# A large expert asks for its width once instead of three times, on TensorE's instruction stream

## What is computed

```python
logits = xf @ w_router + b_router              # 264 tokens of width 1024 (the meta tokens' rows are dropped)
top_val, top_idx = top_k(logits, 4)            # 4 of 32 experts for each token
gates = softmax(top_val)
# for each expert e, over the tokens that chose it:
gt  = minimum(x @ w_gate[e] + b_gate[e], 7)
up  = clip(x @ w_up[e] + b_up[e], -7, 7)
hdn = (up + 1) * gt * sigmoid(1.702 * gt)
out += gate * (hdn @ w_down[e] + b_down[e])
```

## Time and profile before

| what | us |
| --- | --- |
| median of 3 runs | 1245.64 (1241.58 to 1249.92) |
| the profiled execution | 1245.33 |
| its span, first to last instruction | 1243.4 |
| TensorE busy | 1160.7 |
| VectorE busy | 448.6 |
| ScalarE busy | 197.8 |
| mean granted TensorE clock | 0.977 |

### The profile page before, as it was taken

One profiled execution on the slowest core, in us unless ns is written; L12 is line 12 of the kernel. 1 busy time (PEld: TensorE's weight loads), 2 busy tenths in 40 slices (PEclk: granted clock), 3 DMA queues, 4 the chain that ended last, 5 costly groups with the idle time before them and its releaser, 6 DMA issues.

```text
span 1243.4 us, 20526 instructions
## 1 busy us (share of the span) xinstructions
PE 1160.7 (93%) x8392; PEld 550.3 (44%) x8392; DVE 448.6 (36%) x1031; ACT 197.8 (16%) x435; POOL 5.8 (0%) x34
## 2 busy tenths in 40 slices
PE   8999989999999979898999999999999999999886
PEld 6888767774334323232333433333343334343333
DVE  2999998214332323121311233111232212222224
ACT  2234504121110111111110011100111001111012
POOL 1000000000000000000000000000000000000000
PEclk9999999999989999989999999999999899999989
DMA  9641328936989999999999999999999999999993
GB/s 393 239 173 68 144 110 332 370 144 253 381 357 426 427 426 425 427 427 424 426 426 427 425 426 425 427 425 402 427 426 427 424 427 388 429 425 425 429 425 153
DMA packets 37074, 452.62 MB, mean 364 GB/s; under 512 B 5112, under 2 KB 5656, under 8 KB 10080
## 3 DMA queue, kind: packets, MB, share of 16 engines
q1 hardware_dynamic: 35344, 449.02, 86.5%
q10 hardware_dynamic: 1616, 1.82, 0.4%
HBM read 443.57 MB, written 7.25 MB: 363 GB/s over the span
## 4 chain that ended last, share of the span: by engine, by line
PE 55%; DMA 29%; DVE 13%; issue 1%; DVEq 1%; ACT 0%; POOL 0%; SPq 0%; POOLq 0%; ACTq 0%
DMA ring<-in_w_experts 28%; PE ps L1597 23%; PE ps L1630 9%; DVE acts L794 5%; PE ps L1348 3%; PE ps L1523 2%; PE ps L1640 2%; PE ps L1322 2%; PE ps L1564 2%; PE ps L1645 2%; PE ps L1579 2%; DVE acts L889 1%; PE ps L1652 1%; PE ps L1464 1%; PE ps L1620 1%
## 5 line engine op out<-in xcount | busy, mean ns | idle before, releaser
L1597 PE MATMUL ps<-ring,extra 128*64 128x512 f32 x1824 | 415.4, 609 | 18.6 <-DMA ring<-in_w_experts 18.1
L1597 PEld LDWEIGHTS ps<-ring,extra 128*64 128x64 f32 x1824 | 128.8, 140 | 292.1 <-issue 256.3
L1630 PE MATMUL ps<-ring,extra 128*32 128x256 f32 x3072 | 189.3, 388 | 18.7 <-DMA ring<-in_w_experts 18.4
L1630 PEld LDWEIGHTS ps<-ring,extra 128*32 128x32 f32 x3072 | 91.6, 111 | 111.6 <-issue 37.3
L1119 DVE TENSOR_TENSOR acts<-ps,acts 128x528 f32<-128x528 f32 x68 | 47.8, 707 | 252.9 <-PE ps L1645 232.1
L1124 DVE TENSOR_SCALAR extra<-ps 128x512 f32<-128x512 f32 x32 | 22.1, 692 | 216.5 <-PE ps L1597 216.5
L794 DVE SCALAR_TENSOR_TENSOR acts<-ring,small,acts 128x256 f32<-128x256 f32 x224 | 91.4, 478 | 1.1 <-ACT acts L500 1.1
L1348 PE MATMUL ps<-acts,ring 128*128 128x280 f32 (+1 forms) x320 | 75.3, 395 | 0.3 <-ACT ring L573 0.3
L1348 PEld LDWEIGHTS ps<-acts,ring 128*128 128x128 f32 x320 | 60.6, 190 | 14.1 <-issue 1.0
L1348 PE MATMUL ps<-acts,extra 128*128 128x280 f32 x256 | 61.3, 400 | 1.9 <-DVE acts L776 1.9
L1133 DVE TENSOR_SCALAR extra<-ps 128x512 f32<-128x512 f32 x32 | 22.1, 689 | 100.9 <-PE ps L1597 83.1
(11 more groups left out here) (315 smaller groups left out, 854.5 us busy)
## 6 DMA issues: line engine op xcount, KB each, us to landing
ring<-in_w_experts SPq DMA_DIRECT2D x192, 2048.0 KB, 28.9
ring<-in_w_in_t SPq DMA_DIRECT2D x5, 2048.0 KB, 20.9
extra<-in_w_in_t SPq DMA_DIRECT2D x4, 2048.0 KB, 10.9
extra<-in_w_out_t SPq DMA_DIRECT2D x4, 1024.0 KB, 5.9
ring<-in_w_out_t SPq DMA_DIRECT2D x4, 1024.0 KB, 6.1
ring<-in_state_t SPq DMA_DIRECT2D x8, 512.0 KB, 8.8
ring<-dtx_rows SPq DMA_DIRECT2D x8, 512.0 KB, 8.2
out_ssm_s_t<-ring SPq DMA_DIRECT2D x8, 512.0 KB, 8.0
```

What stands on the lines that cost most here:

```text
L1597: hs.append(MM(dst, src[:, o:o + HALF], weight(w, p, k, 512 * h_, 512), start=(fresh and kk == 0), stop=(kk == KT - 1), skip_group_check=T ...
L1630: hs.append(MM(dst, src[:, o:o + QUAR], weight(w, p, k, 256 * q, 256), start=(fresh and kk == 0), stop=(kk == KT - 1), skip_group_check=True))
```

## The change

In a large expert that has a small one behind it, everything from the gate to the down products is put into one function of the width, `whole(n)`, and the width is asked for once. In expert 0, which has a large one behind it, the questions stay as they were. In a small expert, the gather, the turn of its own hidden rows, the slot pick and the turn of the next one's inputs are put into one function `prepare(n)` of the next one's width, asked for once; the operations and waits keep their order. Only TensorE's stream changes.

```diff
-                by_width(count, gate_up)
-                if i == 0:
+                def rest(n):
+                    pe.wait_ge(ev["s_ready"], i + 2)
+                    pe.wait_ge(ev["y_back"], i * 2 + 64)
+                    gather_s()
+                    turn_hidden(n, i * 2)
+                    pe.wait_ge(ev["p_ready"], i + 1)
+                    if i == 1:
+                        pe.wait_ge(ev["acc_done"], back_no(i) + 4)
+                    pick_slots()
+                    pe.wait_ge(ev["xg_out"], i * 2 + 4)
+                    turn_s(xg, 2, ev["xt_done"])
+                    down_of(n, i * 2, w)
+
+                def whole(n):
+                    gate_up(n)
+                    rest(n)
+
+                if following is None:
+                    by_width(count, whole)
+                else:
+                    by_width(count, gate_up)
                     find_order()
                     pe.wait_ge(ev["xg_out"], 2)
-                pe.wait_ge(ev["s_ready"], i + 2)
-                pe.wait_ge(ev["y_back"], i * 2 + 64)
-                if following is None:
-                    gather_s()
-                else:
+                    pe.wait_ge(ev["s_ready"], i + 2)
+                    pe.wait_ge(ev["y_back"], i * 2 + 64)
                     by_width(following, lambda n: gather(n, True))
-                by_width(count, lambda n: turn_hidden(n, i * 2))
-                pe.wait_ge(ev["p_ready"], i + 1)
-                if i == 0:
+                    by_width(count, lambda n: turn_hidden(n, i * 2))
+                    pe.wait_ge(ev["p_ready"], i + 1)
                     pe.wait_ge(ev["order_ready"], 1)
-                elif i == 1:
-                    pe.wait_ge(ev["acc_done"], back_no(i) + 4)
-                pick_slots()
-                if following is None:
-                    pe.wait_ge(ev["xg_out"], i * 2 + 4)
-                    turn_s(xg, 2, ev["xt_done"])
-                else:
+                    pick_slots()
                     pe.wait_ge(ev["hdn_ready"], i * 2 + 2)
                     by_width(following, turn_next(i))
-                by_width(count, lambda n: down_of(n, i * 2, w))
+                    by_width(count, lambda n: down_of(n, i * 2, w))
                 pe.wait_ge(ev["ht_ready"], i * 2 + 2)
...
                 pe.wait_ge(ev["s_ready"], i + 2)
+
+                def prepare(n):
+                    if following is None:
+                        gather_s(False)
+                    else:
+                        gather(n)
+                    pe.wait_ge(ev["hdn_ready"], i * 2 + 2)
+                    turn_s(hdn, 0, ev["ht_done"])
+                    pe.wait_ge(ev["acc_done"], back_no(i) + 4)
+                    pick_slots()
+                    if following is None:
+                        pe.wait_ge(ev["xg_out"], i * 2 + 4)
+                        turn_s(xg, 2, ev["xt_done"])
+                    else:
+                        turn_next(i)(n)
+
                 if following is None:
-                    gather_s(False)
+                    prepare(1)
                 else:
-                    by_width(following, gather)
-                pe.wait_ge(ev["hdn_ready"], i * 2 + 2)
-                turn_s(hdn, 0, ev["ht_done"])
-                pe.wait_ge(ev["acc_done"], back_no(i) + 4)
-                pick_slots()
-                if following is None:
-                    pe.wait_ge(ev["xg_out"], i * 2 + 4)
-                    turn_s(xg, 2, ev["xt_done"])
-                else:
-                    by_width(following, turn_next(i))
+                    by_width(following, prepare)
                 down_s(i * 2, w)
```

## The result

The changed kernel takes 1262.43 us (median of 4 runs, 1251.94 to 1267.56) beside 1245.59 us for the kernel before: a ratio of 1.0134, interval 1.0104 to 1.0164, so 16.8 us and 1.3% slower. The forecast was 1243 in 1236 to 1255; what came is the rival "the cover runs out", worked out as 1264. The profiled execution is the shortest of the four (1251.94 us, span 1250.0, mean granted clock 0.985).

The account below looks back on a forecast made before the run. The prediction took the experts' weight stream, 424 to 427 GB/s, as the bound, with the engine behind only in wide stretches. 1245.3 - 4.1 + 1 + 1 = 1243.2, with the runs' median 0.3 higher; forecast 1243, range 1236 to 1255.

Parts of the forecast that it names:

- the cover runs out: Rival: stalls with half clock make narrow pairs 56.2 us, leaving 22.9 us of lag at the end; 1264 us, chance 0.13.
- The bound and the mechanism: Whole kernel: weight stream bounds, branches cost 0, jumps past the next instruction block stall, 1.75 to 2.97 us in 12 experts.
- First term, the early gain: Around 352 us: without expert 1's stall before its gather, a buffer frees earlier and the dry stream closes; gain 4.1 us.
- Second term, the middle: Narrow and wide pairs: narrow pairs with stalls still make good a wide pair's 14.4 us lag; +1 us (0 to 5).
- The 4.6 us in hand before the stream stops: Behind expert 24: a pair lands 12.5 us after issue, 7.9 with an empty queue, so 4.6 us of slack.
- from 3.0 us a stall on: The rival's threshold: from this stall length two narrow pairs no longer make good a wide one.
- Third term, the end: Experts 26, 28 and 30: three stalls, some 6 us, may make the engine later than the stream; +1 us (0 to 4).

Follow-up runs that it names:

- e2: The kernel before with only the small experts' half of the change; large ones ask as before: 1243.59 us, ratio 0.9988.
- e8: The kernel before with the large experts' gate and up products cut into parts, no jump passing over more than 128 instructions: 1240.68 us, ratio 0.9961.
- e7: The kernel before with never-executed matmuls added, so narrow experts from 4 on jump some 500 instructions ahead of the gather: 1255.78 us, ratio 1.0116.
- e3: The kernel before with the large experts' half of the change in expert 1 only: 1242.24 us, ratio 0.9995.
- e12: The changed kernel with the width test's bound at 256 slots, so every large expert takes the narrow version: 1241.34 us, ratio 0.9977.
- e5: The kernel before with the large experts' half of the change in experts from 14 on only: 1265.95 us, ratio 1.0197.
- e4: The kernel before with the large experts' half of the change in experts 1 to 10 only: 1243.31 us, ratio 1.0000.
- e9: The kernel before with the width test's bound at 320, above the declared 264, so every large expert is worked as narrow: 1233.92 us.
- e11: The kernel before with the width test's bound at 256 slots, so every large expert takes the narrow version: 1243.07 us, ratio 0.9982.
- e13: The kernel before with short jumps in the large experts' gate and up products plus the small experts' half of the change: 1241.33 us, ratio 0.9972.

## Why the prediction was wrong

**The bound and the mechanism** were right. The stream was the bound with the engine close behind. A taken branch costs nothing visible by itself (e2, and e8 with more of them), a long jump waits for its block (e7, e8), and the new stalls lie ahead of the small expert's first products, none ahead of a gather. The Trainium skill, "Runtime: NRT & Kernel Launch", Instruction fetch mechanics, says that a taken branch to a target outside the window of two blocks has to wait for the target's block. The runs agree: waits behind 6 of 13 jumps over 280 instructions (1.1 blocks), behind all 11 over some 500 in e7, and none in e8.

**First term, the early gain.** Forecast 4.1 us, with SP's issue near 349. In place of the earlier trace rows stands

```profile
347.16 0.34 SPq L398 DMA_DIRECT2D ring<-in_w_experts  x1
```

8.1 us earlier and before the queue was empty; the gather started right behind the up products. The stretch lost 6.1 us less, of which 1.7 went again behind expert 12. The term was right in its sign, but e3 could not show it in the time.

**Second term, the middle: this is the step that failed.** "Before, two narrow pairs regained 20.5; now 14.4 to 16.8. That just suffices before the next wide one", and +1 us was taken. The traced execution lost 15.7 us more stream behind the wide experts. What the pairs regained, measured: 55.6 + 61.2 = 116.8 us for the two pairs ahead of expert 18, so 118.2 - 116.8 = 1.4 us regained of 14.4; and 55.8 + 57.1, so 5.3 regained ahead of 24. Four things were mis-sized or left out:
- Waits for issue per pair: 1.8 to 3.0 forecast; 4.6, 6.3, 3.8 and 3.7 found. The second wait behind a landing near a block's end was thought of for the last experts only ("perhaps a second wait"). A wait within the small expert came behind six of the twelve landings.
- The lower clock next to the waits. It was put into the rival alone, on the word of expert 26, where a 1.75 us wait had no such fall. The pair of expert 16, with a clock of 0.94, has 2.3 us of it: 61.2 is 48.9, 6.3 of waits, 3.7 of the next point and 2.3 more. That of expert 20, also 0.94, has 55.8 - 48.9 - 3.8 = 3.1.
- The small expert ahead of a wide one gathers and turns twice as much. The second gather block is 2.9 us, the turns and the wait for their input 0.8 to 0.9. The 48.9 us came from a pair with a narrow one behind it. So 3.7 of the 20.5 us in hand were never there, and of the 6.1 us that seemed left over after the wide pair's 14.4 only 2.4 were. The trace of the kernel before shows it as well: its pair 16 and 17, from 755.56 to 812.41, takes 56.9 us, of which 2.6 are a wait for weights and 1.4 the half clock behind it; 52.9 remain. First these rows of before, then those of after, ahead of a narrow expert and ahead of wide 18:

```profile
755.56 1.07 PE L1579 MATMUL ps<-acts 32*64 32x512 f32 x4
...
787.86 3.29 PE L1630 MATMUL ps<-ring,extra 128*32 128x256 f32 x32 [2.56 <-DMA ring<-in_w_experts]
...
800.53 5.81 PE L1564 MATMUL ps<-acts 128*64 128x512 f32 x24
```

```profile
750.22 2.94 PE L1564 MATMUL ps<-acts 128*64 128x512 f32 x12
...
754.06 0.66 PE L1322 MATMUL ps<-small,extra 128*128 128x128 f32 x4
...
807.50 5.81 PE L1564 MATMUL ps<-acts 128*64 128x512 f32 x24
...
814.79 1.06 PE L1322 MATMUL ps<-small,extra 128*128 128x128 f32 x8 [0.51 <-ACT extra L654]
```

- The 4.6 us in hand before the stream stops. The pair read there was issued at 1043.5 us, within the stretch in which the stream of the kernel before already ran at 368 GB/s. Behind 18 and 24 nothing was in hand.

With 2.4 us in hand for two pairs even the forecast's own two stalls (3.6 to 6 us) were too many, and the rival's point of decision, "from 3.0 us a stall on", lay in truth near 1.2. e12 and e5 show that this is where the time went: without the wide experts 48.2 us of stalls cost nothing, and the change from expert 14 on alone costs 22.5 us.

**Third term, the end.** +1 forecast, 0 found: the last products still wait for the last pair.

**The rival that came** had its price nearly right for a partly wrong reason. It took every stall as one long one with a half clock (56.2 us a pair); the four pairs measured are 57.4 in the mean, two waits each in three of them. But it gave this lag to the end, 22.9 us, where the run had it as dry stretches of the stream, 7.6 us more behind expert 18 and 6.4 behind 24, and the engine was not late at the end. That the median, 1262.4, lies so near to 1264 is in part luck: the traced execution has 6.6 us of the loss, the others the rest, at lower clocks. The chance of 0.13 was too low: it was judged against a cover read from one undisturbed pair, never added up for the pair that ends in a wide expert.

What stays open: what decides whether the lower clock comes with a wait; why the stream runs dry behind expert 12 in e4, e8 and the changed kernel and not in the kernel before; and why e9 ends 9 us ahead of e11, of which the early stretch explains 5.2.

## What to carry to other kernels

Count the instructions that a run-time branch jumps over, not the branches: five questions with short jumps (e8) were better than one with a long one, and cutting a 280-instruction jump into parts of at most 128 removed every stall. Before calling a new stall covered, add up the time in hand over the whole cycle in which it must be regained, here one wide pair and the two narrow ones ahead of the next, from the timeline of each, the preparation for the wide one included. And a branch whose bound lies outside the register's declared range may not be in the program at all: look at the number of instruction blocks before reading an experiment.

## What was not expected of the hardware

A jump over some 500 instructions can stall twice. At the landing it costs 1.80 to 2.26 us, and in half of the cases 1.76 to 4.59 us within the next 4.2 us of work, where in the case looked at one 16.4 KB block begins to come at most 2.9 us before the engine goes on. The second wait ends 5.1 to 6.2 us after the first product behind the landing in all 32 cases that seven traces show behind jumps this long, so its length is what the work in between leaves of that. In e12, whose code is laid out alike, the waits come after the same numbers of matmuls as in the changed kernel (4.14 us in expert 17's bias, 5.15 in expert 15's first products), so it seems to be where the landing lies in its block that matters and not the moment. Jumps of 128 instructions and fewer had no wait in e8 and one, of 0.4 us, in e13. Stalls and half clock together, 48 us of one and a mean clock of 0.95 to 0.97, cost a stream-bound kernel nothing (e12); without time in hand behind the wide experts 40 us of stalls came with 6.6 us more span in the traced execution and 16.8 us in the median (the changed kernel).
